# Gate stores on SyncE, fetched rows later in the searches, two tile closings in the next layer's front

## The reference

```python
def peer(h, w_q, key1, key2, u_tab, v_tab):
    q = (x @ w_q).reshape(n, PEER_HEADS, 2, PEER_HALF).astype(jnp.float32)
    s1 = jnp.einsum('nhd,kd->nhk', q[:, :, 0], key1.astype(jnp.float32))
    s2 = jnp.einsum('nhd,kd->nhk', q[:, :, 1], key2.astype(jnp.float32))
    t1, i1 = lax.top_k(s1, PEER_TOPK)
    t2, i2 = lax.top_k(s2, PEER_TOPK)
    ...
    top, pos = lax.top_k(cand, PEER_TOPK)
    idx = jnp.take_along_axis(cand_idx, pos, axis=-1)
    g = jax.nn.softmax(top, axis=-1)
    ...
        a = jnp.einsum('thkd,td->thk', u_tab[ib], xb)
        w = (jax.nn.gelu(a.astype(jnp.float32)) * gb).astype(xb.dtype)
        return jnp.einsum('thk,thkd->td', w, v_tab[ib])
    ...
x = post_norm_residual(x, peer(h, ...), gate2, ln2_g, ln2_b)   # LayerNorm(alpha*x + gate*y)
```

## Time and profile before

| what | us |
|---|---|
| three timed runs, median | 4029.91 (4017.49 to 4030.64) |
| profiled execution | 4024.53 |
| its span, first to last instruction | 4022.7 |
| TensorE busy | 3611.7 (90%) |
| VectorE busy | 2808.4 (70%) |
| ScalarE busy | 844.9 (21%) |
| mean granted TensorE clock | 0.936 of full speed |

### The profile page before, as it was taken

One profiled execution on the slowest core, in us unless ns is written; L12 is line 12 of the kernel. 1 busy time (PEld: TensorE's weight loads), 2 busy tenths in 40 slices (PEclk: granted clock), 3 DMA queues, 4 the chain that ended last, 5 costly groups with the idle time before them and its releaser, 6 DMA issues.

```text
span 4022.7 us, 38562 instructions
## 1 busy us (share of the span) xinstructions
PE 3611.7 (90%) x12502; PEld 2166.3 (54%) x12502; DVE 2808.4 (70%) x6216; ACT 844.9 (21%) x2201; POOL 1630.9 (41%) x1410
## 2 busy tenths in 40 slices
PE   8899778998879999999987977899977899999996
PEld 2335434687768844444435543458866784444442
DVE  0238985889666675666674897688967668666668
ACT  0101421116543200000002142111655320000000
POOL 2224652522353224555520466152226321455553
PEclk9899689999889999999998968899988999999998
DMA  7877874888799978999974687388879997899995
GB/s 269 284 250 269 285 266 153 305 334 294 259 381 353 382 275 350 413 413 414 407 283 161 257 286 271 134 322 321 288 247 399 368 359 292 336 413 413 414 413 231
DMA packets 420760, 1263.24 MB, mean 314 GB/s; under 512 B 37121, under 2 KB 140289, under 8 KB 383697
## 3 DMA queue, kind: packets, MB, share of 16 engines
q0 software_dynamic: 198912, 721.61, 47.8%
q1 hardware_dynamic: 103312, 455.21, 29.6%
q10 hardware_dynamic: 118336, 83.97, 6.5%
HBM read 1173.81 MB, written 86.84 MB: 313 GB/s over the span
## 4 chain that ended last, share of the span: by engine, by line
PE 39%; DVE 21%; DMA 20%; issue 7%; POOL 6%; ACT 4%; ACTq 3%; SPq 0%; DVEq 0%
PE P L814 11%; DMA ring<-in_peer_v_dram,eidx 9%; DMA ring<-in_peer_u_dram,eidx 9%; PE P L789 7%; POOL ring L568 6%; DVE ring L1155 6%; PE P L842 5%; PE T L826 3%; ACTq L1003 3%; PE P L646 2%; PE O L604 2%; PE V L604 2%; PE O L842 1%; PE V L842 1%; DVE h L1173 1%
## 5 line engine op out<-in xcount | busy, mean ns | idle before, releaser
L568 POOL DMA_INDIRECT ring<-in_peer_u_dram,eidx x768 | 943.6, 1229 | 1250.5 <-DVE ring L1155 689.8
L1155 DVE SCALAR_TENSOR_TENSOR ring<-ring,h 128x1024 f32<-128x1024 f32 x768 | 921.7, 1222 | 262.3 <-DMA ring<-in_peer_u_dram,eidx 219.4
L842 PE MATMUL P<-w_ring,area 128*128 128x512 f32 x2048 | 933.4, 599 | 33.3 <-DVE area L1329 31.7
L568 POOL DMA_INDIRECT ring<-in_peer_v_dram,eidx x512 | 603.8, 1179 | 883.3 <-DVE late L1173 518.4
L814 PE MATMUL P<-hT,w_ring 128*128 128x256 f32 x4096 | 934.1, 386 | 0.0
L814 PEld LDWEIGHTS P<-hT,w_ring 128*128 128x128 f32 x4096 | 784.9, 195 | 104.4
L842 PEld LDWEIGHTS P<-w_ring,area 128*128 128x128 f32 x2048 | 391.0, 192 | 536.8 <-issue 536.7
L1173 DVE SCALAR_TENSOR_TENSOR h<-ring,dots,h 128x1024 f32<-128x1024 f32 x254 | 325.9, 1283 | 159.8 <-DMA ring<-in_peer_v_dram,eidx 148.2
L1173 DVE SCALAR_TENSOR_TENSOR late<-ring,dots,late 128x1024 f32<-128x1024 f32 x254 | 325.4, 1281 | 11.3
L789 PE MATMUL P<-hT,w_ring 128*128 128x128 f32 (+1 forms) x1024 | 287.3, 443 | 3.0 <-issue 2.2
L842 PE MATMUL O<-w_ring,qT 128*128 128x512 f32 x512 | 261.5, 592 | 0.0
(11 more groups left out here) (216 smaller groups left out, 3578.1 us busy)
## 6 DMA issues: line engine op xcount, KB each, us to landing
w_ring<-in_peer_uT_dram SPq DMA_DIRECT2D x128, 1024.0 KB
w_ring<-in_peer_vB_dram SPq DMA_DIRECT2D x128, 1024.0 KB
ring<-in_w_mod_dram POOLq DMA_DIRECT2D x96, 512.0 KB, 5.8
w_ring<-in_peer_wq_dram SPq DMA_DIRECT2D x64, 512.0 KB, 5.7
h<-acts_d SPq DMA_DIRECT2D x64, 512.0 KB
w_ring<-in_w_in_dram SPq DMA_DIRECT2D x48, 512.0 KB, 7.7
gate_d<-area ACTq DMA_DIRECT2D x48, 512.0 KB
gate_d<-hT ACTq DMA_DIRECT2D x48, 512.0 KB
```

Source lines behind the costliest of these rows:

```text
L568: pool.indirect_dma_start(out=ring[:, b, :], out_offset=None, in_=tables["uv".index(phase)], in_offset=bass.IndirectOffsetOnAxis(ap=eidx[: ...
L842: mm = pe.matmul(bank[ACC[2 * t + half]][:, :], w, uv_ring[:, b // 2 % (WR // 2), b % 2, half * 512:(half + 1) * 512], start=b == 0, stop= ...
L1155: dve.scalar_tensor_tensor(ring[:, b, :], ring[:, b, :], 1.0, h2[:, k, :], ALU.mult, ALU.mult, accum_out=dots[:, k, row:row + 1]).then_inc ...
```

## The change

Four things are done.

1. The stores of the gate parts leave ScalarE's program and enter SyncE's, in a new function `store_gates`. `gates_with(i)` gives the parts that are stored behind u load i, and behind v load i - 64 for i from 64 on: the part whose last chunk stands at block b goes with i = (b + 9) // 2. SyncE waits until the part's last two chunks have been copied.
2. `CHUNK_BLOCKS` and `SLOT_BLOCKS` change: tile 3's chunks run over blocks 43 to 71 (before 42 to 68), tile 4's over 74 to 97 (before 71 to 96), tile 1's over 106 to 121 (before 101 to 122). Slots of tile 4 stand at block 72 (69), of tile 1 at 104 (99). ScalarE's `top_softmax(3)` stands at block 30 (35) and `gelu_dots(1)` at block 102 (97).
3. In the searches of tiles 3 and 4 VectorE takes a row of tile 1 in each second step, 11 instead of 22 in each. Ten follow with tile 3's last one-hots, then 18 in a heap, and 78 (before 74) with tile 4's one-hots. With tile 1's one-hots come 16 rows of tile 0 (before 32), and the other 16 in a heap behind.
4. At the end of layer 0 VectorE multiplies the gate into all three dense tiles (`gated_sum`) but closes tile 3 only. Tiles 4 and 1 are closed in layer 1's prompt front, behind `take_qk`. Each tile has its own place in `h2` for the sum. Since these places are also used by the attention's transposed probabilities (`pT`), ScalarE waits for the closings once, behind its copy of the prompt's queries.

```diff
-SLOT_BLOCKS = {40: 3, 69: 4, 99: 1}
-CHUNK_BLOCKS = [(3, 42, 27), (4, 71, 26), (1, 101, 22)]
+SLOT_BLOCKS = {40: 3, 72: 4, 104: 1}
+CHUNK_BLOCKS = [(3, 43, 29), (4, 74, 24), (1, 106, 16)]
...
+def gates_with(i):
+
+    after = []
+    for k, first, blocks in CHUNK_BLOCKS:
+        for q in range(SUB // QUAD - 1, CHUNKS, SUB // QUAD):
+            after.append(first + blocks * q // CHUNKS)
+    return [s for s, b in enumerate(after) if (b + 9) // 2 == i]
...
+                def store_gates(part):
+
+                    n, q = divmod(part, SUBS // len(V_DENSE))
+                    for last in (4 * q + 2, 4 * q + 3):
+                        job = ("g", V_DENSE[n], last)
+                        sp.wait_ge(emptied[BANK[job]], emptied_at(job, l))
+                    for h in range(2):
+                        sp.dma_start(gate_d[l].rearrange("(c h) p s n -> h s p c n", h=2)[h, part],
+                                     gate_st[part % 2][:, :, h * P:(h + 1) * P]).then_inc(gate_out[part % 2], 16)
...
                     sp.dma_start(uv_ring[:, i % (WR // 2)], peer_uT[l, i]).then_inc(block_full[i % (WR // 2)], 16)
+                    for part in gates_with(i):
+                        store_gates(part)
...
                     queries(g, 0)
+                    if l and g == "P":
+
+                        act.wait_ge(x_done, x_at(l, 0))
...
-                        if col == SUB // QUAD - 1:
-                            act.wait_ge(emptied[BANK["g", k, q - 1]], emptied_at(("g", k, q - 1), l))
-                            act.wait_ge(emptied[BANK[job]], emptied_at(job, l))
-                            for h in range(2):
-                                act.dma_start(gate_d[l].rearrange("(c h) p s n -> h s p c n", h=2)[h, s],
-                                              gate_st[s % 2][:, :, h * P:(h + 1) * P]).then_inc(gate_out[s % 2], 16)
...
+                    if l and not latent:
+
+                        for t in range(1, len(V_DENSE)):
+                            close_tile(t, l - 1)
...
                 for i in range(2 * PH + 6):
-                    dot_rows(1, i, i + 1)
+                    dot_rows(1, i // 2, (i + 1) // 2)
                     choosing(3, i)
                 slots_out(3)
                 for i in range(2 * PH + 6):
-                    dot_rows(1, 22 + i, 23 + i)
+                    dot_rows(1, 11 + i // 2, 11 + (i + 1) // 2)
                     one_hots(3, i)
                     choosing(4, i)
                 slots_out(4)
                 for i in range(10):
                     one_hots(3, 22 + i)
-                    dot_rows(1, 44 + i, 45 + i)
+                    dot_rows(1, 22 + i, 23 + i)
+                dot_rows(1, 32, 50)
                 for i in range(CHUNKS):
                     one_hots(4, i)
-                    dot_rows(1, 54 + 74 * i // CHUNKS, 54 + 74 * (i + 1) // CHUNKS)
+                    dot_rows(1, 50 + 78 * i // CHUNKS, 50 + 78 * (i + 1) // CHUNKS)
                 slots_out(1)
                 for i in range(CHUNKS):
                     one_hots(1, i)
-                    add_rows(0, PV_EARLY + i, PV_EARLY + i + 1)
+                    add_rows(0, PV_EARLY + i // 2, PV_EARLY + (i + 1) // 2)
+                add_rows(0, PV_EARLY + CHUNKS // 2, PV_LATE)
...
                 for t in range(len(V_DENSE)):
-                    close_tile(t)
+                    gated_sum(t)
+                    if l == DEPTH - 1 or t == 0:
+                        close_tile(t, l)
```

More of the change, by code:

```diff
@@ L490, in _ @@
                     sp.dma_start(uv_ring[:, i % (WR // 2)], peer_vB[l, i]).then_inc(block_full[i % (WR // 2)], 16)
+                    for part in gates_with(KEYS // 2 + i):
+                        store_gates(part)
                     if i == 1:
@@ L1017, in _ @@
                             top_softmax(1)
-                        if b == 35:
+                        if b == 30:
                             top_softmax(3)
@@ L1021, in _ @@
                             top_softmax(4)
-                        if b == 97:
+                        if b == 102:
                             gelu_dots(1)
@@ L1131, in expert_weights, with finish_tile @@
                     link(dve.tensor_tensor(dots[:, k, :], dots[:, k, :], gsm[:, k].rearrange("p h j -> p (h j)"), ALU.mult))
-                def finish_tile(k, total):
+                def finish_tile(k, total, layer):
                     link(dve.scalar_tensor_tensor(x[:, k, :], x[:, k, :], ALPHA, total, ALU.mult, ALU.add))
@@ L1138, in finish_tile @@
                     dve.tensor_tensor(x[:, k, :], x[:, k, :], row3[:, 2, :], ALU.add).then_inc(x_done, 1)
-                    dve.wait_ge(x_done, x_of(l, k))
+                    dve.wait_ge(x_done, x_of(layer, k))
                 def finish_gathered(k):
@@ L1331, in weights_T, with gated_sum @@
                                       gate_in[b // 8 % 2][:, 0:ACT_SUBS, b % 8, :], ALU.mult).then_inc(w_ready, 1)
-                def close_tile(t):
+                def gated_sum(t):
                     for half in range(2):
@@ L1337, in close_tile @@
                         cols = slice(half * 512, (half + 1) * 512)
-                        empty(dve.tensor_tensor(h2[:, 2, cols], ready(job)[:, :], row3[:, 0, cols], ALU.mult), job)
-                    finish_tile(V_DENSE[t], h2[:, 2, :])
+                        empty(dve.tensor_tensor(h2[:, 2 + t, cols], ready(job)[:, :], row3[:, 0, cols], ALU.mult), job)
+                def close_tile(t, layer):
+                    finish_tile(V_DENSE[t], h2[:, 2 + t, :], layer)
                 def rotate(src, dst, t, nh, perm):
```

2 lines of the change are left out of this document (1 added, 1 removed).

## The result

| | before | after |
|---|---|---|
| median of 5 runs | 4028.34 us | 4049.01 us |
| lowest to highest | 4017.49 to 4030.64 | 4043.73 to 4052.79 |
| span of the profiled run | 4022.7 us | 4051.0 us |

The ratio is 1.0055, 95% interval 1.0039 to 1.0071: about 22 us slower, where 53 us faster was forecast. The range (3930 to 4012) does not hold it.

A forecast was written before the change was run, and what follows sets the result against it. TensorE should set the time but rests in the u sweeps, waiting for VectorE and ScalarE; transfers bind tile 4's stage. 18.5 us a layer, 37 for both, plus 16 from the closings, 53 off: 3977 us, range 3930 to 4012.

The forecast's parts named there:

- VectorE's waits go: First u sweep: moving rows later removes TensorE's waits for VectorE, 7.05 us before tile 3's slots and 13.6 us more.
- ScalarE's 42.4 us of stalls lose their cause: u sweep: with the gate stores on SyncE, the cause of TensorE's six waits for gate copies goes, 42.4 us together.
- tile 1's chunks: Late in the u sweep: denser chunks want gate buffers back sooner, 5 us a layer lost, bounds 0 and 24.
- the 33.5 us: u sweep's end at 1357.8 instead of 1391.3: 33.5 us a layer won, before the later stores' costs.
- Only TensorE's lag is gone: Tile 4's chunks: the stage keeps its length, 162 us, but TensorE finishes at 1225, just after VectorE at 1224.
- The junction: From u to v sweep: the last gate store comes later, beside a heap of 16 rows; loss 10 us, bounds 2 and 20.
- The closings: Between the layers: closing two tiles later brings the second layer's first score 16 us earlier, once.
- Rival 2: u sweep: transfers bind, removed waits return as waits for rows and u blocks; only 16 us stay, 4014; chance 0.15.
- Rival 1: Tile 1's chunks and start of v: later stores cost nothing, 79 us won, 3951; chance 0.22.
- Rival 3: u sweep: u loads stand behind slow gate stores in one queue, 67 us slower, 4097, at half that 4037; chance 0.08.
- the ten waits: First u sweep before the change: TensorE's waits for VectorE and ScalarE, read as 64 us together.

The follow-up runs named there:

- early_tail: The changed kernel with gate stores one u load earlier on SyncE and the heap of 16 rows moved into the v sweep: 0.9855 of the kernel before.
- act_tail: The changed kernel with the gate stores back on ScalarE and the heap of 16 rows moved into the v sweep: 0.9944 of the kernel before.
- early_tail_third: The changed kernel with stores one u load earlier, the heap of 16 rows in the v sweep and a third gate buffer: 0.9798 of the kernel before.
- after_tail: The changed kernel with only the heap of 16 rows moved into the v sweep: 0.9965 of the kernel before.

## Why the prediction was wrong, step by step

- **VectorE's waits go: right.** 0.53 us at 1013.21 is all that is left of them, and VectorE was done with tile 4's one-hots at 1225, forecast 1224:

```profile
1224.45 0.68 DVE L1334 TENSOR_TENSOR row<-qT,cst 128x512 f32<-128x512 f32 x1
```

- **"ScalarE's 42.4 us of stalls lose their cause": the step that failed.** The cause seen was ScalarE's blocked queue, and it did go. But the prediction gave the stores a new place 8.7 us behind the last copy (measured 8.2) and costed it only in tile 1's chunks, where it was right in size (waits of 2.07, 1.93, 2.01 and 0.55 us, 6.6 in all, forecast 5). In tiles 3 and 4 a buffer is wanted again as soon: 21 us after the last copy in tile 3 (1018.72 to 1040.00), 18 in tile 4 (1167.16 to 1184.93). The store of part 5 took 32 us to free it, and stores took 27 to 29 us to land in the full stretch of early_tail (last section). TensorE waited 63 us for gate copies there, where the sum had no term for a late buffer. The experiments bear the cause out: an earlier store is worth 45 us, a third buffer 40. They also bound it: with the stores on ScalarE the changed kernel has 61.6 us (70.5 in act_tail) of such waits too, so the late stores did not add 63 us to the kernel, they kept the u sweep from getting shorter. Its last block was done 1.3 us earlier than before, in place of 28.5 (33.5 less 5). That the 33.5 us were there to be had, early_tail_third shows: it is done with the u sweep at 1356.17, forecast 1357.8, though by another mix of waits.
- **"Only TensorE's lag is gone": wrong for the same reason.** The tile 4 stage was taken to keep its length "since transfers fill it", with ScalarE's waits merely replaced. TensorE took the last of tile 4's chunks at 1248.77, 24 us behind VectorE, where the sum had 1225. Before, the lag was 9.45 us. So here, too, the late buffers stood behind it. Of the 38 us by which v starts later than forecast (1411.58 against 1373.5), these are 24.
- **The junction: right mechanism, size just over its upper bound.** Forecast 10, bounds 2 and 20, measured 21.60 less 0.73, 20.9. That is 11 of the 38 us. The heap was named in the prediction, but as something that would delay the store by little; after_tail shows that 15.7 us of the 20.9 were the heap's, and the other 5 go with the early store.
- **The closings: right**, 16 us forecast, 16.5 in the front's length, 0.9949 alone. The first score stands at 2134.89, 34.7 us behind v's end, before 49.3.
- **Rival 2, the waits that go come back, is what the u sweep did**, and it had too small a chance: inside the sweep nothing was won. It named rows and u blocks as the new waits, and they were for gate buffers. Its 4014 was too low by the junction: twice 20.9 us on top make 4056, measured 4049. Its idea about the rows held with two buffers only.
- **Rival 1, the later stores cost nothing, had 3951**: early_tail_third, in which early stores, a third buffer and no heap take that cost away, measured 3948.5.
- **Rival 3 had the price and the wrong victim.** It reckoned 24 us for a part and 4 for the load behind, where packets of fetched rows go between. Measured from issue to landing in early_tail, 1025 to 1225, medians of 8 stores each: 27.1 and 28.9 us, against 5.3 and 7.5 in 930 to 1020. The rival asked whether a u load comes late by that (lead 27 us) and found it unlikely. It never asked the same of the gate buffer, whose lead is 18 to 21 us and which needs the store, not the load. Its argument against, that SyncE never waited for its queue, was true only of a SyncE that issued no stores.
- **A slip in the reading of before:** the ten waits make 63 us (7.05, 13.6 and 42.4), not 64. Nothing hangs on it.

## What to carry to other kernels

When a store is moved to another engine's program, its lateness is paid by whoever fills the buffer next: take the time from the last write of a buffer to the first write of its next use, and set against it the new place plus the landing time in the fullest stretch, for every stage that recycles it, not just the densest. Work taken out of a loop and done in a heap is also a heap of fetches: put it where no transfer on the critical chain is queued. And a wait removed ahead of a stretch with DMA share 1.0 bought nothing here while two gate buffers were the limit, since its bytes moved into that stretch. Lift such a limit before you judge the move.

## What the runs showed of the hardware

- A 512 KB gate store takes 5.3 to 7.5 us to land where the row queue is light (share of queue 0 0.20) and 27 to 29 us where it is heavy (0.65). The rows are of early_tail, 930 to 1020, then 1025 to 1225:

```profile
q0 software_dynamic: 1510, 5.53, 19.8%
...
w_ring<-in_peer_uT_dram SPq DMA_DIRECT2D x10, 1024.0 KB, 7.0
gate_d<-area SPq DMA_DIRECT2D x6, 512.0 KB, 5.3
gate_d<-hT SPq DMA_DIRECT2D x4, 512.0 KB, 7.5
```

```profile
q0 software_dynamic: 14393, 52.42, 64.8%
...
w_ring<-in_peer_uT_dram SPq DMA_DIRECT2D x15, 1024.0 KB, 21.4
gate_d<-area SPq DMA_DIRECT2D x8, 512.0 KB, 27.1
gate_d<-hT SPq DMA_DIRECT2D x8, 512.0 KB, 28.9
```

  The bytes of all queues in the second stretch, 80 MB in 200 us, are 400 GB/s; at that rate a store's own 512 KB would take 1.3 us, an estimate, so nearly all of the 27 us is time in which the engines serve others, the u loads and stores ahead in the same queue among them (a u load lands in 21.4 us there, against 7.0). The Trainium skill, DMA: Bandwidth & Descriptors, Queues, rings and completion order, has each engine take turns between queues packet by packet; these landings agree with it, but they do not separate such turns from the transfers ahead in the same queue.
- The issuing queue of SyncE blocks as ScalarE's did: the issue of one part's stores took 15.55 us in after (1046.60) and 22.39 in early_tail_third (1134.90), ScalarE's up to 13.23. Everything behind it in that program is then late, transfers that are needed first included.
